# A backbone kernel's even input stage: how the adaLN rows are summed, and how its loops are written

## The reference, cut to what matters

```python
sh1, sc1, g1, sh2, sc2, g2 = adaln(silu_c, ada_w[layer], ada_b[layer])        # cond @ w + b, 6 x 1024 columns, two layers
csh1, ...                  = adaln(silu_cc, ada_w[layer], ada_b[layer])       # the same for the context's vector
u = a @ w_in                                                                  # 768 tokens x 1024 -> 5680 columns
conv_in, z, v, o, dt_raw, ig_raw, fg_raw = split(u)
conv_out = silu(dwconv(conv_in, conv_w, conv_b))                              # 3 taps along the tokens, 2560 channels
xs, B, C, q, k = split(conv_out)
dt = softplus(dt_raw + dt_bias); dA = dt * -exp(a_log); ig = ig_raw + b; lf = log_sigmoid(fg_raw + b)
```

## Time and profile before

| | us |
|---|---|
| median of 3 runs (lowest, highest) | 2019.71 (2018.65, 2025.02) |
| profiled execution | 2019.79 |
| its span | 2018.1 |
| PE busy | 1682.3 (83%) |
| PE weight loads busy | 1007.5 (50%) |
| DVE busy | 681.0 (34%) |
| ACT busy | 528.7 (26%) |
| POOL busy | 276.7 (14%) |

### The profile page before, as it was taken

The page is one execution under the profiler, slowest core; times in us unless marked ns, Lnnn a source line. Parts: engine busy times, 40 slices in busy tenths (PEclk is TensorE's granted clock), DMA queues, the critical chain, the costliest instruction groups (busy, mean ns, idle before and its releaser), DMA issues. The chain is left out here.

```text
span 2018.1 us, 18719 instructions
## 1 busy us (share of the span) xinstructions
PE 1682.3 (83%) x6575; PEld 1007.5 (50%) x6575; DVE 681.0 (34%) x1248; ACT 528.7 (26%) x1031; POOL 276.7 (14%) x289
## 2 busy tenths in 40 slices
PE   4999979999987997699957999908969999399960
PEld 2555544434336775345435777604435544377740
DVE  1123239000005876343341111114546634311114
ACT  4122121110007663544101111114236621011111
POOL 0000000000005865112001001011000000011001
PEclk9999999999997998799978999959979999599985
DMA  8345434665539884723107999962030012489963
GB/s 311 115 154 170 169 126 166 248 221 224 189 127 304 236 242 133 285 94 125 52 26 299 350 351 360 353 227 94 11 84 1 1 65 94 169 292 347 348 258 117
DMA packets 154321, 380.38 MB, mean 188 GB/s; under 512 B 14161, under 2 KB 87409, under 8 KB 134289
## 3 DMA queue, kind: packets, MB, share of 16 engines
q1 hardware_dynamic: 128680, 285.45, 41.6%
q0 software_dynamic: 20208, 75.15, 9.9%
q10 hardware_dynamic: 5369, 18.95, 2.3%
HBM read 312.19 MB, written 67.32 MB: 188 GB/s over the span
## 5 line engine op out<-in xcount | busy, mean ns | idle before, releaser
L1772 PE MATMUL ex_ps_gu<-ex_wgu,ex_xT 128*128 128x256 f32 x1152 | 260.9, 385 | 9.4 <-DMA ex_wgu<-in_moe_w_gate_dram 5.7
L604 PE MATMUL ie_pu<-ie_w_zvo,aT_even 128*128 128x512 f32 x576 | 254.2, 599 | 8.1 <-ACTq L703 8.1
L1772 PEld LDWEIGHTS ex_ps_gu<-ex_wgu,ex_xT 128*128 128x128 f32 x1152 | 220.8, 193 | 59.7 <-issue 17.7
L565 PE MATMUL ie_pu<-aT_even,ie_w_conv 128*128 128x512 f32 (+1 forms) x640 | 209.0, 487 | 7.6 <-PE ie_px L578 4.0
L604 PEld LDWEIGHTS ie_pu<-ie_w_zvo,aT_even 128*128 128x128 f32 x576 | 108.4, 191 | 153.7 <-issue 153.7
L1441 PE MATMUL po_ps_y<-po_w,po_yT 128*128 128x512 f32 x384 | 170.9, 604 | 4.2 <-ACT po_w L1319 2.2
L565 PEld LDWEIGHTS ie_pu<-aT_even,ie_w_conv 128*128 128x128 f32 x640 | 120.8, 190 | 94.6 <-issue 86.8
L1790 PE MATMUL ex_ps_d<-ex_wd,ex_hT 128*128 128x512 f32 x288 | 131.2, 598 | 3.4 <-DVE ex_hT L1875 2.1
L1441 PEld LDWEIGHTS po_ps_y<-po_w,po_yT 128*128 128x128 f32 x384 | 73.7, 195 | 93.9 <-issue 90.2
L737 DVE SCALAR_TENSOR_TENSOR ie_y<-ie_pu,pcol,ie_y 128x255 f32<-128x255 f32 x80 | 47.4, 614 | 168.3 <-ACT ie_y L687 165.1
L1871 DVE TENSOR_TENSOR ex_hid<-ex_hid,ex_ps_gu 128x256 f32<-128x256 f32 x36 | 15.1, 421 | 241.4 <-PE ex_ps_gu L1772 241.4
(11 more groups left out here) (422 smaller groups left out, 2250.3 us busy)
## 6 DMA issues: line engine op xcount, KB each, us to landing
ex_wgu<-in_moe_w_gate_dram SPq DMA_DIRECT2D x36, 1024.0 KB, 10.0
ex_wgu<-in_moe_w_up_dram SPq DMA_DIRECT2D x36, 1024.0 KB, 11.8
ex_wd<-in_moe_w_down_dram SPq DMA_DIRECT2D x36, 1024.0 KB, 8.8
ie_w_conv<-in_ada_w_dram SPq DMA_DIRECT2D x20, 1024.0 KB, 7.4
y<-ex_y ACTq DMA_DIRECT2D x36, 512.0 KB, 9.4
ie_w_zvo<-in_ev_w_in_dram SPq DMA_DIRECT2D x6, 2048.0 KB, 8.6
rc_mt<-ac_rows SPq DMA_DIRECT2D x12, 1024.0 KB, 6.1
ie_w_conv<-in_ev_w_in_dram SPq DMA_DIRECT2D x10, 1024.0 KB, 6.3
```

The lines of the kernel that those rows point to most:

```text
L565: last = nc.tensor.matmul(pu[t][:, a:b], w_conv[h][:, k, t * P:(t + 1) * P], aT[:, k, a:b], start=(k == 0), stop=(k == KD - 1))
L604: last = nc.tensor.matmul(pu[bank // 2][:, bank % 2 * BANK:(bank % 2 + 1) * BANK], aT[:, k, T * P:(T + 1) * P], w_zvo[b % 2][:, k, :], sta ...
L1772: last = nc.tensor.matmul(ps_gu[s][part][:, 0:FF], xT[s][:, k, :], wgu[s][:, part, k, :], start=(k == 0), stop=(k == KD - 1))
```

## The change

Diff, cut to its core; lines that only rename or drop semaphores are left out.

Setup: the order of the units, where the sums stand, and which pairs are turned and which are stored. `ada_sum` are two SBUF tiles of 128x2048; `sel[:, cond, :]` is zero but for a column of ones at `cond`.

```diff
-    ADA_SLOTS = (ADA_UNITS - 1) * KD
+    ADA_ORDER = (0, 1, 3, 4, 2)
+    ADA_SLOTS = len(ADA_ORDER) * KD
+    SUM_AFTER = (7, 13, 19, 25, 31)
+    TURNED = (0, 1, 2, 3, 4, 8, 9)
+    STORED = range(4, PAIRS)
...
+        sel, acc1 = sb("sel", [P, 2, 32]), sb("acc1", [P, ADA_W])
-                 y_all[...][:, 0:ADA_W], tok_all[...][:, 0:ADA_W]]
+                 y_all[...][:, 0:ADA_W]]
+        ada_sum = [tok_all[...][:, 0:ADA_W], acc1[:, :]]
+        px_flat = [px[t][:, :, :, :].rearrange("p a b c -> p (a b c)") for t in range(2)]
```

```diff
+            def load_z(b):
+                sp.wait_ge(z_done, (b - 1) * NT)
+                sp.dma_start(w_zvo[b % 2][:, :, :], ...).then_inc(z_loaded[b % 2], 16)
...
-            load_ada(3)
-            for n_z in range(GROUPS):
-                if (n_z + 1) % NT == 0 and (n_z + 1) // NT + 1 < ZBLOCKS:
...
-                for n in ada_after(n_z):
-                    if n + 4 < ADA_SLOTS:
-                        sp.wait_ge(ada_done, n + 1)
-                        load_ada(n + 4)
+            for n in range(ADA_SLOTS):
+                v, k = n // KD, n % KD
+                if k == 5 and v + 2 < ZBLOCKS:
+                    load_z(v + 2)
+                if n + 3 < ADA_SLOTS:
+                    sp.wait_ge(ada_step, 2 * n + 2)
+                    load_ada(n + 3)
...
+            sp.wait_ge(ada_taken, 4)
             # stores of the units' rows, then the waits for y_cleared and ada_taken
```

```diff
+            def sum_ada(v):
+                pe.wait_ge(ada_step, 2 * KD * (v + 1))
+                if v >= 2:
+                    pe.wait_ge(ada_taken, v - 1)
+                for cond in range(2):
+                    for j in range(4):
+                        last = nc.tensor.matmul(ada_acc[v % 2][32 * j:32 * j + 32, :], sel[:, cond, :], ada_sum[cond][:, j * BANK:(j + 1) * BANK],
+                                                start=(cond == 0), stop=(cond == 1))
+                last.then_inc(ada_summed, 1)
+            project(0)
+            project(1)
+            pe.wait_ge(tail_taken, 1)
+            turn(0)
+            for p in range(2, PAIRS):
+                project(p)
+                turn(p - 1)
             for n_z in range(GROUPS):
...
+                if n_z == 0:
+                    turn(PAIRS - 1)
+                if n_z in SUM_AFTER:
+                    sum_ada(SUM_AFTER.index(n_z))
+                if n_z == GROUPS - 3:
+                    # wait ada_taken 5, four transposes of ada_row[2]
+                if n_z == GROUPS - 2:
+                    # wait packs_ready 1 and mcol_ready 2, twelve transposes of the packs
-                for n in ada_after(n_z):
...
-                    ada_slot(nc, ada_acc[u % 2], kit.ccol, k, ada_w[n % 4]).then_inc(ada_done, 1)
```

```diff
+                if p == 2:
+                    soft(0, 3, 1)
+                if p == 4:
+                    soft(3, 5, 2)
             act.wait_ge(act_needs, 3)
             # seven Exp
-            zvo_out(act, 1, ZITER)
+            for s in range(4):
+                act.sem_inc(z_taken[s], 1)
+            zvo_out(act, 0, ZITER)
```

```diff
+            steps = gates(dve, V, ch)
+            taps(0)
+            for p in range(1, PAIRS):
+                taps(p)
+                to_tokens(p - 1)
+                next(steps)
+            to_tokens(PAIRS - 1)
+            def weigh(n):
+                v, k = n // KD, n % KD
+                dve.wait_ge(ada_loaded[n % 3], n // 3 * 16 + 16)
+                for cond in range(2):
+                    c = kit.ccol[:, k, cond:cond + 1]
+                    if k == 0:
+                        last = TS(ada_sum[cond], ada_w[n % 3], c, None, ALU.mult)
+                    else:
+                        dve.wait_ge(ada_step, 2 * n + cond - 1)
+                        last = V.scalar_tensor_tensor(ada_sum[cond], ada_w[n % 3], c, ada_sum[cond], ALU.mult, ALU.add)
+                    last.then_inc(ada_step, 1)
...
+            # waits for the last token stores of both buffers
+            for v in range(len(ADA_ORDER)):
+                for k in range(KD):
+                    weigh(v * KD + k)
+                if v == 0:
+                    next(steps)
+                    dve.wait_ge(bias_loaded, 128)
+                take_row(v)          # wait ada_summed v + 1, add the bias row, give ada_taken
+            take_columns(kit, dve, V, 1, ada_acc[1], m_turned, mcol_ready, scaled)
```

More of the change, by code:

```diff
@@ L382, in phase_in_even, with turned_to, times_stored @@
         packs_ready, packs_turned, rows_stored = S("packs_ready"), S("packs_turned"), S("rows_stored")
-        def ada_after(g):
-            done, now = (x * ADA_SLOTS // (2 * GROUPS) * 2 for x in (g, g + 1))
-            return range(done, now)
+        def turned_to(p):
+            return 2 * (TURNED.index(p) + 1)
+        def times_stored(pairs, p):
+            return 16 * len([q for q in pairs if q <= p and q % 2 == p % 2])
         def give_back(pool, i, n):
@@ L475, in gates @@
             dve.sem_inc(act_needs, 1)
+            yield
             V.tensor_copy(packS[0:NDT, :], r["dt"][:, :])
@@ L698, in _ @@
-            for n, (dst, src, func, scale) in enumerate(((r["e"], r["e"], ACT.Exp, 1.0), (g["e"], g["e"], ACT.Exp, 1.0), (sc["na"], sc["alog"], ACT.Exp, 1.0),
-                                                         (r["ln"], r["w"], ACT.Ln, 1.0), (g["ln"], g["w"], ACT.Ln, 1.0))):
-                act.wait_ge(act_needs, 1 if n < 3 else 2)
-                nc.scalar.activation(dst[:, :], src[:, :], func, scale=scale).then_inc(act_gave, 1)
-            for s in range(4):
-                act.sem_inc(z_taken[s], 1)
@@ L704, in _, with soft @@
-            zvo_out(act, 0, 1)
+            def soft(n0, n1, asked):
+                steps = ((r["e"], r["e"], ACT.Exp, 1.0), (g["e"], g["e"], ACT.Exp, 1.0), (sc["na"], sc["alog"], ACT.Exp, 1.0),
+                         (r["ln"], r["w"], ACT.Ln, 1.0), (g["ln"], g["w"], ACT.Ln, 1.0))
+                act.wait_ge(act_needs, asked)
+                for dst, src, func, scale in steps[n0:n1]:
+                    nc.scalar.activation(dst[:, :], src[:, :], func, scale=scale).then_inc(act_gave, 1)
@@ new lines, in _ @@
+            for p in range(PAIRS):
+                h = p % 2
+                if p >= 2:
+                    act.wait_ge(feat_ready, 2 * p - 2)
+                for t in range(2):
+                    c = 2 * p + t
+                    act.wait_ge(u_ready, c + 1)
+                    nc.scalar.activation(y[h][t][:, :], pu[t][:, 0:TOK], ACT.Identity, scale=pcol[:, c + COL_W + NCH:c + COL_W + NCH + 1],
+                                         bias=pcol[:, c + COL_B:c + COL_B + 1]).then_inc(y_begun, 1)
+                if p - 2 in STORED:
+                    act.wait_ge(feat_stored[h], times_stored(STORED, p - 2))
+                if p - 2 in TURNED:
+                    act.wait_ge(turned, turned_to(p - 2))
+                for t in range(2):
+                    c = 2 * p + t
+                    act.wait_ge(y_ready, c + 1)
+                    nc.scalar.activation(feat[h][:, t, :], y[h][t][:, :], ACT.Silu).then_inc(feat_ready, 1)
+                if p == 2:
+                    soft(0, 3, 1)
+                if p == 4:
+                    soft(3, 5, 2)
```

220 lines of the change are left out of this document (92 added, 128 removed).

## The result

Four runs each, on one chip: the changed kernel 1973.97 us (1968.74 to 1980.49), the kernel before 2019.18 (2018.57 to 2025.02). The ratio is 0.9762, 95% interval [0.9728, 0.9795]. On a second chip it was 0.9731 [0.9708, 0.9754] (1973.79 against 2023.48). That is 45 to 50 us faster where 41 were forecast. The profiled execution of after took 1980.49 us (span 1978.8), the slowest of its four runs; that of before had a span of 2018.1. The stage itself became 48.8 us shorter; the profiled span only 39.3, for a reason that stands under the experiments.

A forecast was written before the change was run, and what follows sets the result against it. PE was taken to bound the stage, through its matmuls and few gaps. Start, projections, seam and z/v/o part put the stage end at 560.8 instead of 601.6, so 2019.8 - 40.8 = 1979 us, range 1972 to 2003.

The forecast's parts named there:

- Start: Stage start: the tail's sums move from pu to px, so PE's first projection starts at 56.7 us instead of 59.74.
- Projections: PE's ten projections: 21.18 us each, 23.08 with a turn, 0.43 per loop branch; the last ends at 277.6, 10.2 earlier.
- Seam: Between projections and z/v/o part: DVE's tokens and gates, then ACT's issue; z group 0 at 287.3 us, 16.3 earlier.
- E9: Landmark: end of PE's last projection, 287.8 us before the change, forecast at 277.6.
- Rival (d): Seam: z_taken waits for the whole of the exponentials; 1984 us, inside the forecast's own range, no separate chance.
- The z/v/o part: PE from 287.3 us: 40 slots (37.2) go, five sums (9.3) come; last group ends at 553.7 instead of 591.8.
- DVE in time: z/v/o part: DVE's adaLN work needs 38.2 of 43.7 us per unit, 5.5 to spare, and costs PE nothing.
- (a): z/v/o part: DVE becomes the bound with passes of 4.1 us; 2075 us, 55 later than before; 7%.
- (b): z/v/o part: loads landing in 12.7 us set DVE's pace; 2028 us; 3% slower, 4% for a part near no change.
- (c): z/v/o part: sums a little late, by passes of 2.9 us (1991 us) or DVE starting 10 us later; 14%.
- L1087's rate: Recurrent stage: DVE's 128x1024 product beside POOL's TENSOR_TENSOR took 2158 ns; at that rate the new passes would take 4 us.
- The end: Stage end: after PE's last group 1.2 us to the store's issue, 2.3 to landing, 3.6 to the next stage: 560.8.

The follow-up runs named there:

- Experiment 2: Changed kernel with PE again waiting for its own result behind each projection and turn, constants, no loop: 1973.44 us, ratio 0.9749; stage 499.3.
- experiment 3: Changed kernel with projections 2 to 5 in a two-pass loop: 1968.71 us; with own-result waits and signals behind each projection and turn too: 1973.38.
- experiment 8: Changed kernel with ACT giving z_taken before its wait for the last piece of the gates: 1963.86 us, ratio 0.9706; stage 488.5.
- Experiment 4: Changed kernel with adaLN rows made on PE again in 40 slots, without DVE's passes and the five sums: 2004.43 us, ratio 0.9910; stage 530.0.
- experiment 5: Changed kernel with four more DVE passes of 128x2048 in each adaLN row: 1994.29 us, ratio 0.9855; stage 515.9.
- Experiment 11: Experiment 8's kernel with ScalarE's and GpSimd's last zvo pass written out, plus the last two zvo stores on SP's queue: 1960.48 us, ratio 0.9674.
- experiment 6: Changed kernel with all ten pairs turned and stored again: 1977.29 us, ratio 0.9768; stage 499.1.

## Why the prediction was a little too slow

By its own steps, forecast against the first profiled execution of after. The forecast stage end was 560.8, the measured 552.8, and the sum of the differences is -8.0.

- **Start.** 56.7 forecast, 57.6 measured, +0.9. The wait is gone as forecast, and PE's 0.31 with it; the tail's matmuls began 0.7 later and took 0.7 longer than before. Other executions give 56.0 to 59.0.
- **Projections: the step that failed.** From P0 to the end of the last projection 220.9 were forecast, 213.0 measured, -7.9. "One projection takes 21.18 from start to start, 23.08 with a turn behind it" was carried over from the earlier trace rows. The 0.31 behind a projection, which stands in those very rows with PE's own result as its releaser, was taken for a fixed part of it, and the 0.43 of a loop's branch was the only thing that I let the written-out loop give back. But the diff deletes the waits for own results and the signals behind them (w_free, turn_done). Experiment 2 puts 4.5 of it on the waits; experiment 3 shows that with the signals and the loop as well the whole difference is there (the last turn 222.0 after P0 against 213.0; by the forecast's prices it would be 221.2), and that the loop alone is free.
- **Seam.** 9.7 from E9 to z group 0 forecast, 9.8 measured, by the chain and the releaser forecast. Rival (d) fell: group 0 began while the exponentials ran. What I missed is that this chain was for the most part needless: 6.0 of the 8.4 us went in experiment 8.
- **The z/v/o part.** 266.4 forecast, 263.1 measured, -3.3. A group alone takes 6.88 (48.16 for the seven before the first sum), not the 6.97 that I took from pairs of groups between slots; the 35 groups took 241.5 us, not 243.8. Experiment 4 with its slots has 7.06. The turn and the packs' transposes took 1.3 each, not 1.9, a price that held the waits of the projections, and the row's transposes 0.4, not 0.8; group 0 took 9.4, not 8.7. The 40 slots and five sums were sized right.
- **DVE in time.** The pass was 2.35 for 2.36, TENSOR_SCALAR 1.29 for 1.3, a row 34.15 for 35.6. DVE began at 297.2 instead of 305. PE waited at no sum; (a), (b) and (c) fell. The spare time of 5.5 was a little low: the second row's last pass ends at 376.1 and its sum begins at 382.5, so 6.4; the 9.4 of experiment 5 were over it. L1087's rate of 2158 ns for half the elements did not come, with GpSimd issuing only transfers beside the passes. The Trainium skill, VectorE: DVE Perf Modes (The TRN2 errata), puts an f32 pass over two tensors of 2048 elements at 2.29 us; the trace has 2.35 with 2.26 from start to start. The Trainium skill, SBUF — State Buffer (Who interferes with whom), lets such a pass contend only with GpSimd instructions that read SBUF, and the trace agrees as far as it goes: no run had such an instruction beside these passes.
- **The end.** 7.1 forecast from PE's last group to the next stage, 9.3 measured, +2.2. I read the 3.6 behind SP's rows as the way out of any stage. Experiment 11 shows 1.5 behind an SP store and 5.6 behind a GpSimd store. By these two numbers GpSimd's store at 593.04 would have let the next stage start at about 600.9 before the change too, and by the 8.5 of experiment 6, which stores all pairs as the kernel before does, at 601.5; measured were 601.57. So the modulation rows probably did not set that end; this is worked out, not run.
- **What follows** was carried unchanged, and is unchanged but for the recurrent stage, which takes 168 to 188 us with the clock granted in that execution.

That the profiled execution of after took 1980.49 us, next to the forecast of 1979, is luck: the changed stage was 8.0 us shorter than forecast, and the recurrent stage behind it happened to be 9.4 longer than before.

By landmarks the stage's 48.8 us are 2.1 at the start (P0), 15.1 in the projections (228.1 to 213.0), 6.0 at the seam (15.8 to 9.8) and 26.9 in the z/v/o part (290.0 to 263.1, with 3.0 of turn and transposes moved into it), less 1.3 at the end (8.0 to 9.3). The parts undone alone give 34.7 for the rows, 8.0 for waits, signals and loop on PE, 3.7 to 4.3 for the tail's bank and 3.8 for three turns. These add up to 50 to 51, but they are no account of the 48.8: the seam is not among them, since no experiment put its old order back, and 4 to 5 of the 34.7 are experiment 4's arrangement.

## What to carry to other kernels

An idle time of a few tenths whose releaser is the engine itself is not part of the instruction: count such waits in the diff, with the signals behind them and the loop's way back, and price each; PE idled on them 18 times in this stage, 7.4 us in all. Before moving a wait for a late chain, ask which of the things queued behind it need that chain at all. And when an engine's spare time is read from its waits, take off the round trip that the wait contains (here 2 of 8.4 us, the sum itself), and the slower clock of the engine that then has to wait.

## What was not expected of the hardware

- After PE waits for its own matmuls, it loses about 0.3 us, and about 0.25 more if a signal stands behind the wait (20.65, 20.96, 21.21 us a projection). A loop's way back costs 0.42 behind such a wait and nothing without one (21.95 in the loop and out of it).
- Behind a stage that ends with a store of GpSimd's the next one starts 5.6 us after the landing (6.2 in experiment 6); in experiment 11, with the last store on SP's queue, it was 1.5.
- The same recurrent stage takes 168 to 188 us at a mean granted clock of 0.93 to 0.86, from execution to execution of the same or nearly the same kernel. Between the two profiled executions of the changed kernel it differs by 7.6 us, the whole span by 6.7.
- DVE kept 2.35 us for a pass over 128x2048 with PE full and 225 GB/s of transfers beside it.
